# The token mixers of a hybrid decoder layer: late projection products in whole half tiles, five a chunk, and the other work of TensorE in five runs between them

## The reference

```python
proj = h @ w_in                              # q, k, v, decays, ..., and 3072 columns "gates"
for 128 tokens at a time (a chunk):          # two gated linear attentions (GLA, HGRN2)
    o   = (q * exp(b)) @ state + (scores of q and k inside the chunk, with decays) @ v
    state = state * exp(b_last) + (k * exp(b_last - b)).T @ v
    o   = rms_norm(o) * silu(gate)           # "ya"
for 128 tokens at a time:                    # Mamba-2 state space model (SSD), 16 heads
    w   = exp(b_i - b_j) * (C @ B.T) * dt    # 16 matrices of 128 x 128: "wmat"
    y   = w @ x + (C @ state) * exp(b)       # intra + inter
    state = state * exp(b_last) + (weights * x).T @ B
    y   = rms_norm((y + d * x) * silu(z))    # "yb"
g = sigmoid(proj's gates); x = x + (g0*(ya_gla@w0) + g1*(ya_hgrn@w1) + g2*(yb@w2)) @ w_out
```

## Time and profile before

| what | value |
|---|---|
| median of three runs | 2033.29 us |
| the profiled execution: its time, its span | 2036.86 us, 2034.5 us |
| the stage of the mixers in the span | about 579 to 1082 us |
| TensorE busy over the span | 1921.0 us (94%) |
| VectorE, ScalarE busy over the span | 1449.6 us (71%), 1053.1 us (52%) |
| granted TensorE clock over the span, mean | 0.975 of full speed |

### The profile page before, as it was taken

One profiled execution on the slowest core, in us unless ns is written; L12 is line 12 of the kernel. 1 busy time (PEld: TensorE's weight loads), 2 busy tenths in 40 slices (PEclk: granted clock), 3 DMA queues, 4 the chain that ended last, 5 costly groups with the idle time before them and its releaser, 6 DMA issues. The chain is left out here.

```text
span 2034.5 us, 26573 instructions
## 1 busy us (share of the span) xinstructions
PE 1921.0 (94%) x10542; PEld 1575.9 (77%) x10543; DVE 1449.6 (71%) x1567; ACT 1053.1 (52%) x1250; POOL 218.0 (11%) x176
## 2 busy tenths in 40 slices
PE   6999999999999999999998999995999999999993
PEld 5789888888988777777776888874788888888881
DVE  5967467667326878777775656556889988999975
ACT  5224444544314545444444244323777888878763
POOL 3310000000030000000001000012122222222210
PEclk9999999999999999999998999997999999999997
DMA  5241332423255557646537644543999999999986
GB/s 168 86 145 63 125 99 98 135 94 102 95 157 151 162 152 177 169 128 149 161 118 279 217 195 192 229 170 141 350 376 385 387 385 383 392 387 385 383 343 260
DMA packets 212413, 436.08 MB, mean 214 GB/s; under 512 B 28018, under 2 KB 151042, under 8 KB 184770
## 3 DMA queue, kind: packets, MB, share of 16 engines
q1 hardware_dynamic: 179394, 355.68, 49.9%
q10 hardware_dynamic: 20864, 53.49, 7.5%
q0 software_dynamic: 12032, 25.22, 3.2%
HBM read 369.67 MB, written 81.43 MB: 222 GB/s over the span
## 5 line engine op out<-in xcount | busy, mean ns | idle before, releaser
L1612 PE MATMUL psum<-h_hi,l_hi 128*128 128x512 f32 x384 | 158.2, 412 | 3.3 <-PEq L58 3.3
L1612 PE MATMUL psum<-h_lo,l_hi 128*128 128x512 f32 x384 | 160.7, 418 | 0.0
L1612 PE MATMUL psum<-h_hi,l_lo 128*128 128x512 f32 x384 | 158.1, 412 | 0.0
L2763 DVE TENSOR_TENSOR gu_lo<-up_raw,gu_hi 128x2048 fp32r<-128x2048 f32 x64 | 146.3, 2287 | 13.2 <-ACT gu_hi L2706 13.0
L2706 ACT CAST gu_hi<-up_raw 128x2048 fp32r<-128x2048 f32 x64 | 122.2, 1912 | 34.5 <-PE u_ps L2835 34.4
L1259 ACT COPY l_out<-psum 128x512 f32<-128x512 f32 x48 | 28.2, 587 | 166.3 <-PE psum L1612 161.0
L2479 PE MATMUL mpsum<-y_hi,wb_hi 128*128 128x512 f32 x256 | 103.1, 403 | 9.8 <-DVE y_lo L2237 9.2
L2835 PE MATMUL g_ps<-gu_hi,xeT_hi 128*128 128x512 f32 x256 | 105.3, 411 | 5.9 <-DVE xeT_lo L2772 5.9
L806 DVE TENSOR_TENSOR w_lo<-w_raw,w_hi 128x512 fp32r<-128x512 f32 x90 | 61.9, 689 | 65.3 <-ACT w_hi L662 65.3
L662 ACT CAST w_hi<-w_raw 128x512 fp32r<-128x512 f32 x90 | 55.8, 622 | 91.8 <-PE ps L931 91.3
L2835 PE MATMUL g_ps<-gu_hi,xeT_lo 128*128 128x512 f32 x256 | 101.8, 398 | 0.0
(11 more groups left out here) (471 smaller groups left out, 5393.6 us busy)
## 6 DMA issues: line engine op xcount, KB each, us to landing
up_raw<-moe SPq DMA_DIRECT2D x62, 1024.0 KB, 8.0
gate_raw_a<-moe SPq DMA_DIRECT2D x33, 1024.0 KB, 8.4
gate_raw<-moe SPq DMA_DIRECT2D x33, 1024.0 KB, 8.4
dn_raw_a<-moe SPq DMA_DIRECT2D x31, 1024.0 KB, 7.3
dn_raw<-moe SPq DMA_DIRECT2D x31, 1024.0 KB, 8.0
w_raw<-w_in SPq DMA_DIRECT2D x26, 1024.0 KB, 6.0
l_raw<-w_gates ACTq DMA_DIRECT2D x24, 512.0 KB, 5.0
s_gates<-l_out ACTq DMA_DIRECT2D x48, 256.0 KB, 4.3
```

The source lines that it names most:

```text
L1612: ins = nc.tensor.matmul(psum[:, bank, :], w[t % 2][:, k, :], x[:, k, half * 512:half * 512 + 512], start=i == 0, stop=i == LATE_MM - 1, s ...
L2763: nc.vector.tensor_tensor(gu_lo[p][:], gu_raw[p][:], gu_hi[p][:].bitcast(F32), ALU.subtract).then_inc(gu_ready, 1)
```

## The change

TensorE's order becomes five half tiles of 24 matmuls, whole, and between them five runs of other work. Counted from the chunk's first half tile: behind half h0 `level` 1 and 2, `cb`, `ssm_state(c-1)`; behind h0+1 `level` 3 and 4, the transposes into bT, `ssm_means(c-1)`; behind h0+2 the transposes of x, `level` 5 and 6; behind h0+3 the transposes of k, `o`, `inter`; behind h0+4 `upd(c)`, `intra(c, 0)`, `diagonal(c+1)`, `level(c+1, 0)`, the means of `o`, `intra(c, 1)`. Below, these are run 1 to run 5, and F1 to F5 are the halves ahead of them. The last chunk leaves out its transposes of k, `upd` and the update of the state, which nobody reads. VectorE's and ScalarE's pieces are put in another order; `factors` becomes a function of chunk and level, and `gla_hgrn_out` is split in two.

The diff, cut to the three bodies (the moved functions are unchanged inside):

```diff
 # ScalarE, body(c)
+                late(h0 - 1)
+                for lv in (2, 3, 4):
+                    relative(c, lv)
                 if c:
                     gla_hgrn_scale(c - 1)
-                relative(c, 2)
-                relative(c, 3)
-                relative(c, 4)
                 late(h0)
-                relative(c, 5)
                 if c:
                     ssm_squares(c - 1)
...
                 differences(range(SSM_HEADS // 2))
                 late(h0 + 1)
+                relative(c, 5)
+                relative(c, 6)
+                act.wait_ge(bT_ps_ready, c + 1)
+                if c:
+                    act.wait_ge(hupd_ready, c)
+                nc.scalar.copy(flat(bT[:]), ssm_ps).then_inc(bT_ready, 1)
                 if c:
                     ssm_scale(c - 1)
-                relative(c, 6)
                 differences(range(SSM_HEADS // 2, SSM_HEADS))
+                act.wait_ge(seg_ready, SSM_HEADS * (c + 1))
+                nc.scalar.activation(wmat, wmat, ACT.Exp, scale=-1.0).then_inc(wexp_ready, 1)
...
                 late(h0 + 2)
-                act.wait_ge(seg_ready, SSM_HEADS * (c + 1))
-                nc.scalar.activation(wmat, wmat, ACT.Exp, scale=-1.0).then_inc(wexp_ready, 1)
-                act.wait_ge(bT_ps_ready, c + 1)
-                if c:
-                    act.wait_ge(hupd_ready, c)
-                nc.scalar.copy(flat(bT[:]), ssm_ps).then_inc(bT_ready, 1)
-                act.wait_ge(kT_ps_ready, c + 1)
-                nc.scalar.copy(flat(k_in[b][:]), mid_ps[:, 0:CT * P]).then_inc(kT_ready, 1)
                 late(h0 + 3)
+                if c < LAST:
+                    act.wait_ge(kT_ps_ready, c + 1)
+                    nc.scalar.copy(flat(k_in[b][:]), mid_ps[:, 0:CT * P]).then_inc(kT_ready, 1)
+                    relative(c + 1, 0)
                 act.wait_ge(o_ready, c + 1)
...
                 if c < LAST:
-                    relative(c + 1, 0)
                     relative(c + 1, 1)
-                late(h0 + 4)
 # VectorE, body(c)
-                factors(0)
-                factors(1)
                 if c:
+                    gla_hgrn_state(c - 1)
+                    dve.wait_ge(inter_used, c)
+                    intra_in(c - 1, 0)
                     dve.wait_ge(o_ready, c)
                 diagonal_in()
...
                 scores_in(1)
-                dec(i0 + 5)
-                factors(3)
+                factors(c, 3)
                 if c:
-                    x_weighted(c - 1)
-                    x_in_sum(c - 1)
                     z_gated(c - 1)
-                    late(h0 - 1)
+                scores_in(2)
+                factors(c, 4)
                 dve.wait_ge(bb_loaded, 16 * (c + 1))
                 dve.wait_ge(tok_ready, 1)
                 tt(wd[b][:, 0, :], wmat[:, :, CH - 1], tok[:, c, 0, :], ALU.subtract).then_inc(wdarg_ready, 1)
-                scores_in(2)
-                dec(i0 + 6)
-                factors(4)
-                late(h0)
                 dve.wait_ge(cb_ready, c + 1)
 # TensorE, body(c)
-                diagonal(c)
-                if c:
-                    intra(c - 1, 1)
-                fill(SLOT)
-                level(c, 0)
-                fill(SLOT)
+                fill(LATE_MM)
                 level(c, 1)
-                fill(SLOT)
                 level(c, 2)
...
                 ins.then_inc(cb_ready, 1)
-                fill(SLOT)
-                level(c, 3)
                 if c:
                     ssm_state(c - 1)
-                fill(SLOT)
-                if c:
-                    ssm_means(c - 1)
+                fill(LATE_MM)
+                level(c, 3)
+                level(c, 4)
                 pe.wait_ge(cbm_ready, c + 1)
...
                 intra(c, 0)
-                fill(SLOT)
-                pe.wait_ge(state_ready, c + 1)
+                if c < LAST:
+                    diagonal(c + 1)
+                    level(c + 1, 0)
+                    pe.wait_ge(state_ready, c + 1)
                 pe.wait_ge(sq_ready, c + 1)
...
                 ins.then_inc(ms_ready, 1)
-                fill(SLOT)
+                intra(c, 1)
```

More of the change, by code:

```diff
@@ L1364, in _ @@
             relative(0, 1)
-            late(4)
             for c in range(NCH):
                 body(c)
+            late(PREFIX + PER_CHUNK * NCH - 1)
             gla_hgrn_scale(LAST)
@@ L1445, in x_weighted, with gla_hgrn_mean, gla_hgrn_out @@
                 tt(xdt[:], xdt[:], wd[c % 2][:, 1, :].unsqueeze(2).to_broadcast([P, SSM_HEADS, SSM_HD]), ALU.mult).then_inc(xw_ready, 1)
-            def gla_hgrn_out(c):
+            def gla_hgrn_mean(c):
                 dve.wait_ge(rs_ready, c + 1)
                 tt(ya, o_ps.rearrange("p (k t) -> p k t", t=CH), ya, ALU.mult).then_inc(o_used, 1)
+            def gla_hgrn_out(c):
                 dve.wait_ge(g_loaded, 32 * (c + 1))
@@ L1452, in gla_hgrn_out, with gla_hgrn_state @@
                 tt(ya, g_in[:], ya, ALU.mult).then_inc(ya_ready, 1)
+            def gla_hgrn_state(c):
+                dve.wait_ge(upd_ready, c + 1)
+                own.link(tt(state[:], state[:], b_in[c % 2][:, :, CH - 1:CH].to_broadcast([P, CT, P]), ALU.mult))
+                tt(state[:], state[:], mid_ps[:, 0:CT * P].rearrange("p (a e) -> p a e", e=P), ALU.add).then_inc(state_ready, 1)
             def ssm_state(c):
@@ L1498, in scores_in @@
                                               v(mask[lv][:]), v(sc_ps[lv % 2])).then_inc(score_ready, 1)
-                dve.wait_ge(qk_loaded[b], 80 * turns(c))
                 i0 = NE * c
-                factors(0)
-                factors(1)
                 if c:
+                    gla_hgrn_state(c - 1)
+                    dve.wait_ge(inter_used, c)
+                    intra_in(c - 1, 0)
                     dve.wait_ge(o_ready, c)
                 diagonal_in()
-                dec(i0 + 3)
-                dec(i0 + 4)
-                if c:
-                    gla_hgrn_out(c - 1)
-                else:
-                    late(3)
                 scores_in(0)
-                factors(2)
+                factors(c, 2)
                 if c:
                     intra_in(c - 1, 1)
+                    gla_hgrn_mean(c - 1)
+                    x_weighted(c - 1)
+                late(h0 - 1)
+                if c:
+                    x_in_sum(c - 1)
+                dec(i0 + 5)
                 scores_in(1)
-                dec(i0 + 5)
-                factors(3)
+                factors(c, 3)
                 if c:
-                    x_weighted(c - 1)
-                    x_in_sum(c - 1)
                     z_gated(c - 1)
-                    late(h0 - 1)
+                scores_in(2)
+                factors(c, 4)
                 dve.wait_ge(bb_loaded, 16 * (c + 1))
@@ L1534, in body @@
                     .then_inc(cbm_ready, 1)
+                dec(i0 + 6)
+                late(h0)
                 if c:
+                    gla_hgrn_out(c - 1)
                     ssm_state(c - 1)
                 scores_in(3)
+                factors(c, 5)
+                scores_in(4)
+                factors(c, 6)
                 dec(i0 + 7)
-                factors(5)
                 late(h0 + 1)
-                scores_in(4)
-                factors(6)
                 dve.wait_ge(xT_ready, c + 1)
@@ L1554, in body @@
                 tt(q_in[b][:, 2:8, :], q_in[b][:, 2:8, :], b_in[b][:], ALU.mult).then_inc(q_dec_ready, 1)
+                dec(i0 + 8)
+                late(h0 + 2)
+                if c:
+                    ssm_out(c - 1)
+                dec(i0 + 9)
+                dec(i0 + 10)
                 dve.wait_ge(wexp_ready, c + 1)
@@ L1558, in body @@
                 tt(w4, w4, cbm[:].unsqueeze(2).to_broadcast([P, SSM_GROUPS, GH, CH]), ALU.mult).then_inc(w_ready, 1)
-                if c:
[L1560 to L1563, removed]
+                late(h0 + 3)
                 dve.wait_ge(small_ready, c + 1)
@@ L1568, in body @@
                 tt(yt[:], inter_ps.rearrange("p (k t) -> p k t", t=CH), eb_in[:], ALU.mult).then_inc(inter_used, 1)
[L1569 to L1574, removed]
+                if c < LAST:
+                    factors(c + 1, 0)
+                    dec(i0 + 11)
+                    factors(c + 1, 1)
+                    dec(i0 + 12)
             project_stored(dve)
@@ L1579, in _ @@
             late(1)
+            for lv in range(2):
+                factors(0, lv)
+                dec(lv + 3)
+            late(3)
             for c in range(NCH):
@@ L1583, in _ @@
                 body(c)
+            dve.wait_ge(inter_used, NCH)
+            intra_in(LAST, 0)
             intra_in(LAST, 1)
@@ L1720, in body @@
                 ins.then_inc(bT_ps_ready, 1)
-                fill(SLOT)
-                level(c, 4)
-                fill(SLOT)
+                if c:
+                    ssm_means(c - 1)
+                fill(LATE_MM)
                 pe.wait_ge(x_loaded, 16 * (c + 1))
```

(13 more changed lines are left out.)

51 lines of the change are left out of this document (25 added, 26 removed).

## The result

The changed kernel takes 2046.55 us (median of 8 runs, 2042.96 to 2049.38); the kernel before, measured beside it, 2035.39 (8 runs). The ratio is 1.0055 with a 95% interval of 1.0038 to 1.0072: 0.55% slower, above the 0.3% that a measurement tells. The forecast was 2027, a little faster than before; the measured time lies on the other side of the kernel before and outside the range up to 2040. The profiled execution took 2047.14 us.

What follows compares the result with a forecast made beforehand. Bound: TensorE, busy 483.5 of 503 us, within a round through eb's load, wmat's landing and ScalarE. Savings 9.0 (rounds) + 1.0 (chunk 0) + 2.4 (last chunk) - 6.0 (clock) = 6.4 us: 2033.3 to 2026.9, range 2010 to 2040.

Steps and rivals of the forecast that it cites:

- chunk 0, to eb of chunk 1: First chunk, wmat early and no round: seven cuts fewer up to its `inter`, partly hidden, save 1 us.
- eb's issue to wmat's landing: SyncE's loads: eb, v and wmat queue up, so wmat lands 27.5 us behind eb's issue, as before the change.
- the round: Loop from one eb load to the next through wmat, ScalarE, F4 and `inter`: 56.2 us without clock falls, against 57.7 before.
- The step that failed: SyncE's queue: issuing wmat about 11 us behind eb doesn't move its landing at 27.5, since v lands only at 13.4.
- The falls of the clock: TensorE at half clock behind gaps of 2.6 to 3.1 us ahead of F4: seven cost 12 us, half counted, 6.
- ScalarE's chain: ScalarE's work from wmat's landing to the copy of half h0+2 that F4 waits for: 15.6 us a round.
- D: Loads of x, z and weights issued beside wmat slow its landing to 18.9 us; 2041 us, chance 0.18.
- E: The same round through wmat without a fall of TensorE's clock; 12.4 us less, 2021 us, chance 0.14.
- A: The round through wmat as summed, with some falls of the clock; 2027 us, 2023 to 2031, chance 0.34.
- C: Nothing measurable: seven clock falls take back 12 of 12.4 us, or TensorE isn't the bound; 2033 us, chance 0.22.
- B: TensorE alone bounds if wmat lands 4 to 5 us sooner; 35 us less, 1998 us, chance 0.12.
- The cuts: Switches on TensorE between late matmuls and other work: 72 fewer at 0.25 us each, 18 us of TensorE's own work.

Runs made afterwards that it cites:

- e5: Changed kernel with v's load issued behind wmat's instead of ahead of it on SyncE; 2047.37 us, 1.007 of the kernel before.
- e2: Changed kernel with SyncE issuing the loads of x and z only when wmat has landed; 2039.41 us, 1.0019 of the kernel before.
- e7: Changed kernel with only ScalarE's copy of bT moved behind the copy of half h0+2 that F4 waits for; 2038.27 us, 1.0025 of the kernel before.
- e3: Changed kernel with wmat's source laid out by chunk, one piece of 8 KB per partition instead of 16 of 512 bytes; 1995.77 us.
- e8: Changed kernel with wmat's source padded so its 512-byte pieces lie 1 KB apart instead of 4 KB; 1998.62 us, 0.9817 of the kernel before.
- e9: Changed kernel with each row of wmat's source 512 bytes longer, so pieces lie 4.5 KB apart instead of 4 KB; 1998.08 us, 0.9829 of the kernel before.
- e4: Kernel before the change with wmat's source laid out by chunk, one piece of 8 KB per partition; 2019.99 us, 0.9925 of the kernel before.
- e1: Changed kernel with ScalarE's copy of bT and wmat's large exponential moved behind the copy F4 waits for; 2018.02 us, 0.9916 of the kernel before.
- e6: Changed kernel with the edits of e3 and e1 together; 1992.77 us, 0.9817 of the kernel before.

## Why the prediction was wrong

The place and the chain were right: VectorE's wait, the three waits of TensorE in their order, ScalarE's copy as the releaser, half clock behind the gaps, and the largest wait ahead of F4. The sum was wrong in size and so in sign. Its terms against the profile, in us:

| term | forecast | measured |
|---|---|---|
| chunk 0, to eb of chunk 1 | -1.0 | +2.8 |
| eb's issue to wmat's landing (first six chunks) | 27.5 | 28.8 |
| landing to F4 | 15.6 | 15.82 |
| F4, run 4, to eb, with half of the falls (0.85) | 13.95 | 14.69 |
| the round | 57.05 | 59.32 |
| eb of chunk 7 to the last late product | 82.65 | 84.1 |

The forecast ones are the prediction's (for the last, 84.2 of before less 2.4, with 0.85). The miss is 3.8 + 6 x 2.27 + 1.45 = 18.9 us, that is from -6.4 to the +12.5 of the stage.

**The step that failed** is the one on the landing: that wmat's later issue "doesn't move this: wmat still is issued before v has landed". It took the three loads for a queue in which wmat's start is v's end. wmat was still issued before v had landed, and yet it landed later: 28.57 us behind eb over seven chunks, where the profile before has 27.39. Of these 1.18 us 0.85 are its later issue (11.48 us behind eb instead of 10.63), and 0.33 its own way from issue to landing (17.10 instead of 16.77). v lands 1.2 us later as well (14.3 us behind eb instead of 13.1), which a queue behind v would give too; e5 speaks against it, since with v behind wmat the landing stayed. That wmat's time runs from its own issue is argued from this; no run moved the issue alone. x and z beside it cost 0.7 to 1.0 us of its own way (e2). Against this stands that without them its own way was 16.15, 0.6 less than before; no run says why. The six rounds have 6 x 1.3 = 7.8 of the 18.9 us from here, the largest part.

**The falls of the clock** were mis-sized: half of seven was counted, six of the seven gaps of 2.94 to 3.05 us were followed by one (chunk 4, with 3.05, was not), and chunks 0 and 6 had one more each. In chunk 4 the way from F4 to eb is 13.19 us, where the prediction's without falls is 13.1; the mean is 1.5 us longer. That is the 0.7 between F4 and eb and about half of the last chunk's 1.45. The rule of the Trainium skill weighed there ("TensorE: Matmul & The Clock Gate", "HAM oscillation"), by which none would come, the traces don't bear out: e7 has falls behind 2.46 us. **Chunk 0**'s wait for a store, 3.13 us with a fall behind it, was not foreseen; it varies from run to run. **ScalarE's chain** is 15.76 to 15.86 us in every chunk, without the two lengths that the prediction gave it: 0.2 more than the 15.6 taken.

**The rivals.** D came nearest (2041 against 2046.55), but not for its own reason alone: x and z are at most 1.0 of the 2.27 us by which a round was missed, and its sign, a wmat that takes over 18.5 us to land, didn't come (18.3 at most). The ring order of the Trainium skill ("DMA: Bandwidth & Descriptors", "Queues, rings and completion order"), read as that later loads of the same queue can't push wmat back, is against e2. The same section of the Trainium skill says that a later descriptor may finish its write before an earlier one, so that reading went beyond the page. E fell with the clock, A by its sum. C was nearly right in its falls, but the loss lies above its 0.3%. B was the case to look at: it said what the change is worth if wmat came 4 to 5 us sooner, 1998; in e3, e8 and e9 it comes 11 to 12 us sooner and the times are 1995.8 to 1998.6. That the number came out so near has luck in it, as the cuts show.

**The cuts** were put too high: 18 us in 72 of 0.25. Between e4 and e3 TensorE's busy time falls by 14.5 us; less the 2.4 put down for the last chunk this leaves 12, 0.17 a cut. Why it isn't 0.25 no run shows. The 24.2 us between the two times hold more than the cuts: TensorE's idle time falls by 4.9 us as well, as the wait of L1675 ends. B's sum had left out the half clock of the kernel before. Without it, in e4, TensorE is busy for 5.6 us less than before (477.84 instead of 483.47), and this stood in for the missing 6.

## What to carry to other kernels

When work of the bounding engine is merged into longer pieces, its cuts are a gain only where nothing else closes the round; write down the chain that runs through the single buffer (here wmat) first, and take out of it what nobody waits for yet, as e1 did. A load that takes more than twice as long as another of the same size (before the change a half of eb, 256 KB, landed in a median of 10.2 us, `k_in` from `s_k_hg`, 256 KB as well, in 4.1) is a question to ask before building on its time: change its layout in memory alone and look. A sum that explains the time of a transfer by its neighbours should be tried by moving a neighbour, before it is used to forecast.

## What was not expected of the hardware

A load of 1 MB whose 128 partitions read the same 16 pieces of 512 bytes lands in a median of 17.6 us with the pieces 4 KB apart, 5.6 with 4.5 KB, 5.9 with 1 KB, and 5.4 as one piece of 8 KB. What in the memory makes 4 KB dear no run shows; for v and x, which are read otherwise, spacing wasn't tried, though both land sooner too when wmat and eb are quick (medians of 8.7 and 10.7 us before the edit, 3.6 and 4.1 in e9).

Gaps of TensorE of nearly one length are followed by half clock or not: 3.05 and 2.54 us by none, 2.94 and 2.46 by at least 3.3 us at 1.2 GHz. In the changed kernel even two waits of 1.57 us for `cbm` part: chunk 4 stays at 2.4 GHz, chunk 6 falls.

```profile
857.55:859.12 1.57, 0.00 (x1) 0.00 (x0) 0.83 (x3) 0.62 (x3) 0.00 (x0) 1.00 1.11 302
859.15:862.50 3.35, 2.35 (x8) 1.04 (x8) 3.35 (x4) 3.32 (x10) 0.00 (x0) 1.00 0.37 97
976.44:978.01 1.57, 0.00 (x1) 0.00 (x0) 0.83 (x3) 0.62 (x3) 0.00 (x0) 1.00 1.14 326
978.25:981.60 3.35, 3.35 (x8) 1.54 (x6) 3.35 (x4) 3.32 (x10) 0.00 (x0) 0.50 0.34 87
```

What decides between them stays open. e6 and e9, which both beat the kernel before by 1.7 to 1.8%, can't be told apart by their intervals; e9's padding together with e1's order wasn't run, nor a second buffer for wmat.
